# A hybrid encoder's first SSD layer with its time steps first, and the weight splits of the middle groups one unit further ahead

## The chip, the cores and the metric
The kernel runs on one core of a Trainium2 chip. The metric is the time of one execution on the device, in microseconds (us). TensorE is called PE in the rows of the profile (PEld is its weight load), VectorE is DVE, ScalarE is ACT, GpSimd is POOL, SyncE is SP.

## What is computed
An encoder trunk of four layers over 256 tokens of 1024 features, all in float32. The token mixers are, in order: a bidirectional Mamba-2 SSD, a short gated convolution, a neighbourhood attention and a second SSD. Each is followed by a dense MLP with squared ReLU, and each sub-layer by a LayerNorm. The SSD mixer, cut to what matters:
```python
zxbcdt = x @ w_in
z, xbc, dt_raw = split(zxbcdt)
xbc = silu(depthwise_conv(xbc, conv_w) + conv_b)
dt = softplus(dt_raw + dt_bias)            # the time steps, 2 directions x 32 heads
y = y_fwd + y_bwd + d_skip * xs            # y_fwd: chunks of 128 tokens, decays exp(cumsum(dt * a))
y = grouped_rmsnorm(y * silu(z), norm_w) @ w_out
```

## The kernel before
**Units.** All weights pass through SBUF in units of 128 x 2048 float32 (1 MB; the unit of the time steps, dt, has 0.26 MB). `plan_units` (L73) gives their order. Of an SSD layer there are, for each of 8 groups g, z(g), bc(g) (the state's two inputs), x(g) and, two groups later, so(g), the rows of the output weights. In the first layer the order is z0, z1, dt, bc0, x0, bc1, x1, z2, bc2, x2, so0, z3, bc3, x3, so1 and so on, units 0 to 14; the second layer has dt first. SyncE loads a unit with two DMAs into one of six raw buffers (RAW), when the unit six before it has been used up.

**Splits.** Every product is made of three in a reduced float32: high x high, high x low, low x high. ScalarE makes a unit's high part (`w_high`, a rounding copy, L1153) in one of five buffers, then VectorE the low part (`w_low`, raw minus high, L1568) in place of the raw unit. Both do it inside their own hand-written orders: `split_to(u)` makes all splits up to unit u that are still open. ScalarE waits for the unit's landing, VectorE for `w_high_done`. TensorE waits for both parts in `weights(u)`. Unit 0 alone is split in two halves with semaphores of their own (`first_high`, `first_low`, L1152, L1565), so that the first z product can begin with half of the weights. The products of one unit are 48 matmuls (L594 and L615), or 24 of 512 columns for so (L775).

**Start of the first layer.** TensorE turns x (L738), ScalarE and VectorE make its high and low parts (L1195, L1671), and TensorE then does z0, z1 with the turns of the parameters between their halves (`turn_ssd_parameters`, L820), dt (`dt_features`, L650), `turn_conv_parameters` (L828), `turn_dt` (L659), the first half of bc0 and so on. VectorE's `time_constants` (L1725 to L1742) are some twenty small dependent instructions that make softplus of dt; they need `a_done`, ScalarE's exponential of the parameter a (L1345), which waits for all parameter loads, SyncE's six and GpSimd's seven. Then come the cumulative sum on TensorE (`cumsum`, L883), its copies and decays, its turn (`cumsum_rows`, L891), a store to DRAM by ScalarE's queue (L1371) and GpSimd's broadcast loads of the decays (`load_decays`, L458).

**A middle group i (3 to 6).** TensorE: z(i), `state_products(i-1)` (L912), `turn_xs(i-1)` (L901), bc(i), `cross_chunk(i-1)` (L923), `scan(i-1)` (L936), x(i), so(i-2), `turn_gated(i-1)` (L947). VectorE: silu of z(i) (L1768), `decayed_products(i-1)` (L1797 to L1807), a split, `join_decays(i)` (L1786), `add_cross(i-1)` (L1817 to L1834), `taps` of bc(i) (L1756), `gate_scan(i-1)` (L1853, L1855), silu of bc(i), `rms_known(i-1)` (a wait for GpSimd's power, L481), a split, taps of x(i), silu of x(i), `gated_low(i-1)` (L1776), and the splits that end the loop. ScalarE: tanh of z(i), copies, a split, `shift_decays(i)` (L1269), `start_conv` of bc(i) (L1240, L1246), a split, tanh, `squares(i-1)` (L1311), decays, `normalise(i-1)` (L1319), start_conv of x(i), decays, a split, tanh, `gated_high(i-1)` (L1329), a split. The turns of the inner bank 1 (turn_xs, cross_chunk, turn_gated) wait for one another's readers, so turn_xs also waits for gated_low.

**How far the splits are ahead** is written out by hand. VectorE in a middle group before:
```python
split_to(names[("z", i)] + 4)
...
split_to(names[("bc", i)] + 4)
...
split_to(names[("x", i)] + 4)
if 2 < i < G - 2:
    split_to(names[("so", i - 2)] + 4)
```
With z3 as unit 11 this is 14 and 15, then 16, then 17 and 18, and for group 4: 19, 20, 21 and 22. In the tail (group 7) VectorE makes the split of so(4)+4 between `decayed_products(7)` and the silu of z(7).

## Time and profile before
| what | value |
|---|---|
| median of 3 runs | 1444.96 us (1442.81 to 1445.54) |
| the profiled execution's own time | 1442.69 us |
| its span, first to last instruction | 1441.0 us |
| TensorE matmuls busy | 1395.6 us, 97% of the span |
| VectorE busy | 1034.3 us, 72% |
| ScalarE busy | 763.0 us, 53% |
| mean granted TensorE clock | 0.993 of 2.4 GHz |
| the chain that ended last | TensorE 67%, VectorE 20%, ScalarE 5%, issue 5% |
| DMA | 266.86 MB, 185 GB/s on average |

A busy share is the time in which an engine had an instruction in work. Matmuls are pipelined and their ends are modelled, so TensorE's share is high wherever it doesn't wait. The share is an average over eight sub-layers (the first SSD layer takes about 250 us); a wait of TensorE is read in the stage where it stands.

### The profile page before, as it was taken

Reading aid. Unit: us, or ns where it says so; the run is one execution under the profiler, and the core shown is the slowest. Engines: PE = TensorE matmul, PEld = TensorE weight load, DVE = VectorE, ACT = ScalarE, POOL = GpSimd, SP = SyncE. Lnnn points to the kernel's source line nnn. Section 1 sums busy time; section 2 is a strip of 40 time slices with the busy share of each in tenths; the row PEclk is TensorE's granted clock in tenths of the full one; section 3 lists DMA queues with packets and bytes.
Section 4 is the critical chain, followed back from the end, with each engine's and each line's share of the span. In section 5 each row is a group of like instructions: output and inputs, shape, how many; then the busy total and the mean of one; then the engine's idle time right before and its main releaser. Section 6 shows DMA issues by size and latency. Waiting matters only on the chain.

```text
span 1441.0 us, 22905 instructions
## 1 busy us (share of the span) xinstructions
PE 1395.6 (97%) x8939; PEld 1261.0 (88%) x8939; DVE 1034.3 (72%) x1357; ACT 763.0 (53%) x1137; POOL 168.5 (12%) x229
## 2 busy tenths in 40 slices
PE   7999998999999999999999999999999999899996
PEld 7899997988889999888899798888998998798885
DVE  4899899666578486655766665656899899866554
ACT  4787776554434335444345444443587777554440
POOL 2121111622320000000000000000011121200000
PEclk9899999999999999999999999999999999999998
DMA  9756663676656556555554455554775664465550
GB/s 286 231 176 203 185 198 109 201 215 199 207 170 232 192 176 205 199 182 199 191 166 133 134 188 190 196 184 142 229 253 176 187 196 147 142 206 200 180 175 30
DMA packets 198474, 266.86 MB, mean 185 GB/s; under 512 B 11800, under 2 KB 167856, under 8 KB 198368
## 3 DMA queue, kind: packets, MB, share of 16 engines
q1 hardware_dynamic: 189008, 237.72, 50.8%
q0 software_dynamic: 9200, 27.55, 6.7%
q8 instruction: 72, 1.18, 0.3%
q14 instruction: 34, 0.28, 0.1%
q10 hardware_dynamic: 160, 0.13, 0.0%
HBM read 264.19 MB, written 1.18 MB: 184 GB/s over the span
## 4 chain that ended last, share of the span: by engine, by line
PE 67%; DVE 20%; ACT 5%; issue 5%; POOL 1%; DMA 0%; DVEq 0%; SPq 0%; ACTq 0%; POOLq 0%
PE y L775 27%; PE acc L594 12%; DVE conv L1756 6%; PE acc L632 6%; PE inner L632 6%; PE acc L615 5%; DVE w_low L1568 5%; PE inner L638 3%; PE acc L638 3%; PE y L615 2%; DVE E L1786 1%; ACT w_high L1153 1%; ACT E L1282 1%; PE inner L738 1%; DVE E L1834 1%
## 5 line engine op out<-in xcount | busy, mean ns | idle before, releaser
L1568 DVE TENSOR_TENSOR w_low<-raw,w_high 128x2048 fp32r<-128x2048 f32 (+1 forms) x226 | 511.0, 2270 | 52.5 <-ACT w_high L1153 40.7
L1153 ACT ACTIVATE w_high<-raw 128x2048 fp32r<-128x2048 f32 (+1 forms) x226 | 427.2, 1897 | 169.4 <-PE y L775 132.1
L775 PE MATMUL y<-w_high,opT 128*128 128x512 f32 x1408 | 397.0, 391 | 0.0
L594 PE MATMUL acc<-xT,w_high 128*128 128x256 f32 x1856 | 342.0, 286 | 1.0 <-DVE w_low L1568 0.8
L775 PEld LDWEIGHTS y<-w_high,opT 128*128 128x128 f32 x1408 | 259.3, 188 | 50.8 <-issue 0.7
L594 PEld LDWEIGHTS acc<-xT,w_high 128*128 128x128 f32 x1856 | 290.7, 193 | 2.8 <-issue 2.2
L594 PE MATMUL acc<-xT,w_low 128*128 128x256 f32 x928 | 263.3, 284 | 0.0
L775 PE MATMUL y<-w_low,opT 128*128 128x512 f32 x704 | 222.7, 390 | 0.0
L1587 DVE TENSOR_TENSOR opT<-conv,opT 128x512 fp32r<-128x512 f32 x56 | 40.4, 721 | 223.5 <-issue 202.2
L594 PEld LDWEIGHTS acc<-xT,w_low 128*128 128x128 f32 x928 | 178.8, 193 | 0.0
L615 PE MATMUL acc<-w_high,xT 128*128 128x256 f32 (+1 forms) x928 | 170.6, 286 | 3.4 <-DVE xT L1671 3.4
L775 PEld LDWEIGHTS y<-w_low,opT 128*128 128x128 f32 x704 | 132.1, 188 | 28.3
L615 PEld LDWEIGHTS acc<-w_high,xT 128*128 128x128 f32 x928 | 145.5, 193 | 4.5 <-issue 4.2
L632 PE MATMUL acc<-xT,w_high 128*128 128x512 f32 x352 | 136.9, 389 | 0.0
L632 PE MATMUL inner<-xT,w_high 128*128 128x512 f32 x352 | 136.9, 389 | 0.0
L615 PE MATMUL acc<-w_low,xT 128*128 128x256 f32 (+1 forms) x464 | 131.6, 284 | 0.0
L440 POOL TENSOR_TENSOR small<-small,minus_half 128x1 f32<-128x1 f32 x16 | 22.0, 1377 | 778.6 <-DVE small L1608 744.0
L1756 DVE SCALAR_TENSOR_TENSOR conv<-conv_pad,ssd_par,conv 128x256 f32<-128x256 f32 x256 | 105.6, 485 | 3.0 <-ACT conv L1246 3.0
L1214 ACT ACTIVATE conv<-acc 128x256 f32<-128x256 f32 x44 | 16.9, 384 | 153.6 <-PE inner L638 153.6
L615 PEld LDWEIGHTS acc<-w_low,xT 128*128 128x128 f32 x464 | 89.4, 193 | 0.0
L638 PE MATMUL inner<-xT,w_low 128*128 128x256 f32 x352 | 86.3, 283 | 0.0
L638 PE MATMUL acc<-xT,w_low 128*128 128x256 f32 x352 | 86.0, 282 | 0.0
(230 smaller groups left out, 1587.2 us busy)
## 6 DMA issues: line engine op xcount, KB each, us to landing
raw<-in_ffn_w_in SPq DMA_DIRECT2D x128, 512.0 KB, 4.7
raw<-in_ffn_w_out SPq DMA_DIRECT2D x128, 512.0 KB, 4.3
raw<-in_ssd_w_in SPq DMA_DIRECT2D x96, 512.0 KB, 5.1
E<-cumsum_dram POOLq DMA_DIRECT2D x32, 512.0 KB, 5.0
raw<-in_ssd_w_out SPq DMA_DIRECT2D x32, 512.0 KB, 4.4
raw<-in_sc_w_in SPq DMA_DIRECT2D x24, 512.0 KB, 4.7
raw<-in_na_w_qkv SPq DMA_DIRECT2D x24, 512.0 KB, 4.6
raw<-in_sc_w_out SPq DMA_DIRECT2D x8, 512.0 KB, 4.2
```

The lines of the kernel that those rows point to most:

```text
L440: nc.gpsimd.tensor_tensor(small[:, 2 + t:3 + t], small[:, t:t + 1], half_neg[:, 0:1], ALU.pow).then_inc(rstd_done, 1)
L594: mm = nc.tensor.matmul(bank[:, c * SEQ:(c + 1) * SEQ][:, span], w[:, col:col + P], xT[:, k, low, span], start=(k == 0 and part == 0), sto ...
L615: mm = nc.tensor.matmul(bank[:, t * width:(t + 1) * width], xT[:, k, low, t * P:(t + 1) * P], w[:, k * width:(k + 1) * width], start=(k == ...
L632: nc.tensor.matmul(wide_of[u][c][:, :], wh[:, col:col + P], xT[:, k, :, :].rearrange("p a b -> p (a b)"), start=(k == 0), stop=False)
L638: mm = nc.tensor.matmul(wide_of[u][c][:, 0:SEQ], wl[:, col:col + P], xT[:, k, 0, :], start=False, stop=(k == KT - 1))
L738: mm = nc.tensor.transpose(bank[:, q * P:(q + 1) * P], xs[:, t, c:c + P], ident[:, :])
L775: mm = nc.tensor.matmul(Y[t][c][:, :], opT[:, o % ACTS, low, k, t * P:(t + 1) * P], w[:, k * D + c * 512:k * D + (c + 1) * 512], start=(fi ...
L1153: nc.scalar.activation(w_high[:, u % SPLIT, c0:k * c], raw[:, u % RAW, c0:k * c], ACT.Copy).then_inc(w_high_done, 1)
L1214: ins = nc.scalar.activation(conv[:, o % 2, c, :], wide_of[names[("fi", b)]][c][:, SEQ:2 * SEQ], ACT.Copy)
L1568: V.tensor_tensor(w_low[:, u % RAW, c0:k * c], raw[:, u % RAW, c0:k * c], f(w_high[:, u % SPLIT, c0:k * c]), ALU.subtract).then_inc(w_low_ ...
L1587: V.tensor_tensor(low, src, high, ALU.subtract).then_inc(op_low, 1)
L1756: ins = V.scalar_tensor_tensor(out=y, in0=pad[:, c % 2, i, q:q + SEQ], scalar=tap(j, q, ct), in1=y, op0=ALU.mult, op1=ALU.add)
```

## The change
In the first SSD layer the unit of the time steps, dt, becomes unit 0 and z0 and z1 units 1 and 2. TensorE does dt first, then z0 and z1 with the turns and the cumulative sum between their halves, then bc0 and x0 whole. SyncE issues the second half of x in front of z0 and the six parameter loads in front of unit 2 rather than unit 3. ScalarE and VectorE follow in the same order; unit 0 is no longer split in halves (the semaphores `first_high` and `first_low`, with the code of `tokens` that waits for them, go). In the middle groups of both layers the three places of splits are z+5, bc+5 and x+5 (group 3: units 14, 15 and 16, then 17, then 18; group 4: 19 and 20, then 21, then 22), and the fourth goes. ScalarE's split before the tanh of x(i) goes with it. In the tail VectorE has one split less, between the products of group 7 and the silu of z(7); it is made at the end of group 6. The diff, with indentation cut:
```diff
@@ -83,14 +83,12 @@
 names = {}
 if kind == "ssd":
     for g in range(G + 2):
-        if g == 0 and j:
+        if g == 0:
             add(names, "dt", j, 0)
         if g < G - 1 and g != 1:
             add(names, "z", j, g)
         if g == 0:
             add(names, "z", j, 1)
-        if g == 0 and not j:
-            add(names, "dt", j, 0)
         if g < G:
             add(names, "bc", j, g)
             add(names, "x", j, g)
...
@@ -369,8 +366,8 @@
 for u in range(len(units)):
     if u == 1:
         sp.dma_start(xs[:, 1, :], x[0, P:2 * P, :]).then_inc(x_landed[1], 16)
+    if u == 2:
         sp.wait_ge(x_landed[0], 16)
-    if u == 3:
         load_parameters(sp, 0, par_landed[0])
     parts, k, n = weight_parts(u)
     if u >= RAW:
...
@@ -645,6 +634,9 @@
     bank = acc_bank((dt_copied, 1))
     n["dt"] += 1
     for k in range(KT):
+        if k % (KT // 2) == 0:
+            for t in range(NT):
+                x_half(0, t, k // (KT // 2))
         col = k * 2 * HEADS
         for part, (w, low) in enumerate(((wh, 0), (wh, 1), (wl, 0))):
             mm = nc.tensor.matmul(bank[0:2 * HEADS, 0:SEQ], w[:, col:col + 2 * HEADS], xT[:, k, low, :],
...
@@ -859,16 +851,11 @@
     if s == 0:
         for t in range(NT):
             turn_x(s, t)
-        bank = None
-        for t in range(NT):
-            bank = project(names[("z", 0)], [t], bank, arriving=(s, t))
-        bank = None
-        for t in range(NT):
-            bank = project(names[("z", 1)], [t], bank)
-            turn_ssd_parameters(t)
         dt_features(names[("dt", 0)])
-        turn_conv_parameters()
+        bank = project(names[("z", 0)], [0])
         turn_dt()
+        project(names[("z", 0)], [1], bank)
+        turn_ssd_parameters(0)
     else:
         head_units(s, [names[("dt", 0)], names[("z", 0)], names[("z", 1)]])
...
@@ -948,30 +935,25 @@
                                          gate_of(m)[:, t * GW + c * P:t * GW + (c + 1) * P], ident[:, :])
         mm.then_inc(op_turned, 1)
-    bank = acc_bank(freed_by("bc"))
-    features(names[("bc", 0)], bank, range(NT), None, [0])
     if s:
+        bank = acc_bank(freed_by("bc"))
+        features(names[("bc", 0)], bank, range(NT), None, [0])
         cumsum()
-    used(features(names[("bc", 0)], bank, range(NT), None, [1]))
-    if s:
+        used(features(names[("bc", 0)], bank, range(NT), None, [1]))
         cumsum_rows()
-        project(names[("x", 0)], range(NT))
     else:
+        bank = project(names[("z", 1)], [0])
+        turn_ssd_parameters(1)
         cumsum()
-        bank = acc_bank(freed_by("x"))
-        features(names[("x", 0)], bank, range(NT), None, [0])
+        project(names[("z", 1)], [1], bank)
+        turn_conv_parameters()
         cumsum_rows()
-        used(features(names[("x", 0)], bank, range(NT), None, [1]))
+        project(names[("bc", 0)], range(NT))
+    project(names[("x", 0)], range(NT))
     project(names[("bc", 1)], range(NT))
     state_products(0)
-    if s:
-        turn_xs(0)
-        project(names[("x", 1)], range(NT))
-    else:
-        bank = acc_bank(freed_by("x"))
-        features(names[("x", 1)], bank, range(NT), None, [0])
-        turn_xs(0)
-        used(features(names[("x", 1)], bank, range(NT), None, [1]))
+    turn_xs(0)
+    project(names[("x", 1)], range(NT))
     project(names[("z", 2)], range(NT))
     cross_chunk(0)
     scan(0)
...
@@ -1145,12 +1127,7 @@
     if u >= SPLIT:
         act.wait_ge(w_used, u - SPLIT + 1)
-    c0 = 0
-    if u == 0:
-
-        c0 = k * c // 2
-        nc.scalar.activation(w_high[:, 0, 0:c0], raw[:, 0, 0:c0], ACT.Copy).then_inc(first_high, 1)
-    nc.scalar.activation(w_high[:, u % SPLIT, c0:k * c], raw[:, u % RAW, c0:k * c],
+    nc.scalar.activation(w_high[:, u % SPLIT, 0:k * c], raw[:, u % RAW, 0:k * c],
                          ACT.Copy).then_inc(w_high_done, 1)
             def finished(u):
...
@@ -1335,40 +1312,44 @@
         tanh_of(bank[:, :], 0.5)
     if s == 0:
+        bank = finished(names[("dt", 0)])
+        nc.scalar.activation(csT[:, :], bank[0:2 * HEADS, 0:SEQ], ACT.Copy).then_inc(dt_copied, 1)
         split_to(2)
-        z_tanh(0)
-        split_to(3)
         for n_dmas, landed in zip(n_par_dmas, par_landed):
             act.wait_ge(landed, 16 * n_dmas)
         for q in range(n_ssd):
             ins = nc.scalar.activation(a_neg[:, q, :], a_neg[:, q, :], ACT.Exp)
         ins.then_inc(a_done, 1)
-        bank = finished(names[("dt", 0)])
-        nc.scalar.activation(csT[:, :], bank[0:2 * HEADS, 0:SEQ], ACT.Copy).then_inc(dt_copied, 1)
-        act.wait_ge(par_done, 2 * n_ssd + 1)
-    first = min(names[("dt", 0)], names[("z", 0)])
-    split_to(first + 3)
+    first = names[("dt", 0)]
+    if s:
+        split_to(first + 3)
     act.wait_ge(dt_biased, mixer + 1)
     nc.scalar.activation(dtt[:, 1, :, :], dtt[:, 0, :, :], ACT.Abs).then_inc(act_step, 1)
     n["step"] += 1
     act.wait_ge(act_step, n["step"])
     nc.scalar.activation(dtt[:, 2, :, :], dtt[:, 1, :, :], ACT.Exp, scale=-1.0).then_inc(dt_exp, 1)
-    split_to(first + 4)
+    split_to(first + (4 if s else 3))
     act.wait_ge(dt_floor, mixer + 1)
     nc.scalar.activation(dtt[:, 6, :, :], dtt[:, 7, :, :], ACT.Ln).then_inc(dt_log, 1)
-    split_to(first + 5)
+    split_to(first + (5 if s else 4))
+    z_tanh(0)
     if s:
-        z_tanh(0)
-    z_tanh(1)
+        z_tanh(1)
     act.wait_ge(ncs_done, mixer + 1)
     nc.scalar.activation(to_end[:, :, :], to_end[:, :, :], ACT.Exp)
     nc.scalar.activation(from_end[:, :, :].rearrange("p t c -> p (t c)"),
                          cs[:, :, :].rearrange("p t c -> p (t c)")[:, HEADS:3 * HEADS],
                          ACT.Exp).then_inc(ends_done, 1)
-    start_conv("bc", 0)
+    if s:
+        start_conv("bc", 0)
     act.wait_ge(cs_rows, mixer + 1)
     act.dma_start(rows_dram[j], csT[:, :]).then_inc(rows_stored, 16)
+    if not s:
+        z_tanh(1)
+        split_to(first + 5)
+        act.wait_ge(par_done, 2 * n_ssd + 1)
+        start_conv("bc", 0)
     split_to(first + 7)
     conv_tanh()
     start_conv("x", 0)
...
@@ -1399,7 +1380,7 @@
             if i == 3:
                 decays(2, early)
                 decays(2, late)
-            split_to(names[("z", i)] + 4)
+            split_to(names[("z", i)] + 5)
             shift_decays(i)
         start_conv("bc", i)
         if i == 2:
@@ -1415,18 +1396,16 @@
             split_to(names[("x", 2)] + 4)
             conv_tanh()
         else:
-            split_to(names[("bc", i)] + 4)
+            split_to(names[("bc", i)] + 5)
             conv_tanh()
             squares(i - 1)
             decays(i, early)
             normalise(i - 1)
             start_conv("x", i)
             decays(i, late)
-            split_to(names[("x", i)] + 4)
             conv_tanh()
             gated_high(i - 1)
-        if i > 2:
-            split_to(names[("so", i - 2)] + 4)
+            split_to(names[("x", i)] + 5)
     copy_cross(G - 2)
     copy_xs(G - 2)
     start_conv("bc", G - 1)
...
@@ -1876,27 +1849,28 @@
             dve.wait_ge(xs_turned, m - 1)
         silu(xsT[:, m % 2, :, :].rearrange("p a b -> p (a b)"), y)
+    def ssd_parameters(q):
+
+        dve.wait_ge(par_turned, q + 1)
+        bank = inner_of[("par", q)]
+        V.tensor_scalar(ssd_par[:, q, 0:TAPS + 1, :], bank[:, 0:(TAPS + 1) * CT]
+                        .rearrange("p (a b) -> p a b", b=CT), 0.5, None, ALU.mult).then_inc(par_done, 1)
+        V.tensor_copy(ssd_par[:, q, TAPS + 1, 0:DI // P],
+                      bank[:, (TAPS + 1) * CT:(TAPS + 1) * CT + DI // P]).then_inc(par_done, 1)
+
+    first = names[("dt", 0)]
     if s == 0:
         split_to(2)
+        dve.wait_ge(a_done, 1)
+        time_constants()
+        ssd_parameters(0)
+        split_to(3)
         silu_z(0)
-        split_to(3)
-        for q in range(n_ssd):
-
-            dve.wait_ge(par_turned, q + 1)
-            bank = inner_of[("par", q)]
-            V.tensor_scalar(ssd_par[:, q, 0:TAPS + 1, :], bank[:, 0:(TAPS + 1) * CT]
-                            .rearrange("p (a b) -> p a b", b=CT), 0.5, None, ALU.mult).then_inc(par_done, 1)
-            V.tensor_copy(ssd_par[:, q, TAPS + 1, 0:DI // P],
-                          bank[:, (TAPS + 1) * CT:(TAPS + 1) * CT + DI // P]).then_inc(par_done, 1)
-        dve.wait_ge(par_turned, n_ssd + 1)
-        V.tensor_copy(sc_par[:, :, :], inner_of[("par", n_ssd)][:, 0:SC_TAPS * KT]
-                      .rearrange("p (a b) -> p a b", b=KT)).then_inc(par_done, 1)
-        dve.wait_ge(par_done, 2 * n_ssd + 1)
-        dve.wait_ge(a_done, 1)
-    first = min(names[("dt", 0)], names[("z", 0)])
-    split_to(first + 3)
-    time_constants()
-    split_to(first + (5 if s else 4))
+        ssd_parameters(1)
+    else:
+        split_to(first + 3)
+        time_constants()
+        split_to(first + 5)
     dve.wait_ge(cs_acc, mixer + 1)
     sums = inner_of[("cs", j)]
     V.tensor_copy(cs[:, :, :], sums[:, 0:NT * 2 * HEADS].rearrange("p (t c) -> p t c", t=NT)).then_inc(cs_copied, 1)
...
@@ -1909,9 +1883,17 @@
                     ALU.add).then_inc(ncs_done, 1)
     if s:
         silu_z(0)
-    silu_z(1)
+        silu_z(1)
+    else:
+        split_to(4)
+        dve.wait_ge(par_turned, n_ssd + 1)
+        V.tensor_copy(sc_par[:, :, :], inner_of[("par", n_ssd)][:, 0:SC_TAPS * KT]
+                      .rearrange("p (a b) -> p a b", b=KT)).then_inc(par_done, 1)
     dve.wait_ge(cs_turned, mixer + 1)
     V.tensor_copy(csT[:, :], inner_of[("cs_rows", j)][0:2 * HEADS, 0:SEQ]).then_inc(cs_rows, 1)
+    if not s:
+        silu_z(1)
+        dve.wait_ge(par_done, 2 * n_ssd + 1)
     split_to(first + 5)
     y = taps("bc", 0)
     split_to(first + 6)
...
@@ -1950,19 +1932,17 @@
             gated_low(1)
             join_decays(2)
         else:
-            split_to(names[("z", i)] + 4)
+            split_to(names[("z", i)] + 5)
             join_decays(i)
             add_cross(i - 1)
             y = taps("bc", i)
             gate_scan(i - 1)
             silu_bc(i, y)
             rms_known(i - 1)
-            split_to(names[("bc", i)] + 4)
+            split_to(names[("bc", i)] + 5)
             silu_x(i, taps("x", i))
             gated_low(i - 1)
-        split_to(names[("x", i)] + 4)
-        if 2 < i < G - 2:
-            split_to(names[("so", i - 2)] + 4)
+        split_to(names[("x", i)] + (4 if i == 2 else 5))
     decayed_products(G - 2)
     y = taps("bc", G - 1)
     join_decays(G - 1)
@@ -1973,7 +1953,6 @@
     silu_x(G - 1, y)
     gate_scan(G - 2)
     decayed_products(G - 1)
-    split_to(names[("so", G - 4)] + 4)
     silu_z(G - 1)
     add_cross(G - 1)
```

## Rows read from the trace of the kernel before
**Rows 1.** Windows, all engines: start:end us, length, busy us (instructions), clock, DMA.
```profile
120.00:180.00 60.00, 59.26 (x432) 55.68 (x431) 52.95 (x82) 46.17 (x96) 11.21 (x12) 1.00 0.62 188
```

**Rows 2.** TensorE's waits, whole span: us in total, times, longest.
```profile
PE inner L901 <- DVE xsT L1768: 5.8, 4, 1.9
...
PE inner L947 <- ACT gate L1319: 1.4, 2, 0.7
```

**Rows 3.** Timeline, VectorE, a middle group: start us, us, line, [idle before <-releaser].
```profile
183.32 0.88 DVE L1776 SCALAR_TENSOR_TENSOR opT<-inner,ssd_par,opT 128x256 fp32r<-128x256 f32 x2
184.11 4.48 DVE L1568 TENSOR_TENSOR w_low<-raw,w_high 128x2048 fp32r<-128x2048 f32 x2
188.51 0.68 DVE L1768 SCALAR_TENSOR_TENSOR ring_c<-tanh,acc 128x512 f32<-128x512 f32 x1
...
203.15 2.29 DVE L1568 TENSOR_TENSOR w_low<-raw,w_high 128x2048 fp32r<-128x2048 f32 x1 [1.45 <-POOL small L481]
...
210.39 0.88 DVE L1776 SCALAR_TENSOR_TENSOR opT<-inner,ssd_par,opT 128x256 fp32r<-128x256 f32 x2
```

**Rows 4.** Timeline, TensorE, where it waits or nearly waits in the first layer.
```profile
122.95 0.44 PE L947 MATMUL inner<-ident,gate 128*128 128x128 f32 x2 [0.72 <-ACT gate L1319]
...
211.63 0.38 PE L901 MATMUL inner<-ident,xsT 128*128 128x128 f32 x2
...
226.29 0.55 PE L901 MATMUL inner<-ident,xsT 128*128 128x128 f32 x3 [1.92 <-DVE xsT L1768]
...
239.77 0.33 PE L947 MATMUL inner<-ident,E 128*128 128x128 f32 x1 [1.33 <-ACT E L1319]
```

**Rows 5.** Timeline, VectorE, the splits of group 3.
```profile
107.71 4.49 DVE L1568 TENSOR_TENSOR w_low<-raw,w_high 128x2048 fp32r<-128x2048 f32 x2
```

**Rows 6.** Timeline, ScalarE, the split behind `gated_high`.
```profile
183.18 1.91 ACT L1153 ACTIVATE w_high<-raw 128x2048 fp32r<-128x2048 f32 x1
```

**Rows 7.** Timeline, VectorE's split and ScalarE's tanh of z in the tail.
```profile
229.42 2.28 DVE L1568 TENSOR_TENSOR w_low<-raw,w_high 128x2048 fp32r<-128x2048 f32 x1
...
229.85 0.60 ACT L1254 ACTIVATE tanh<-acc 128x512 f32<-128x512 f32 x1 [1.35 <-PE acc L615]
```

**Rows 8.** The start: SyncE's and GpSimd's issues (timeline), then one load's us to landing.
```profile
4.38 0.37 SPq L383 DMA_DIRECT2D raw<-in_ssd_w_in  x1
...
6.97 2.03 SPq L353 DMA_DIRECT2D E<-in_ssd_conv_w  x1
...
11.71 0.44 SPq L387 DMA_DIRECT2D raw<-in_ssd_w_in  x1
...
9.83 0.79 POOL L353 DMA_DIRECT2D E<-in_ssd_conv_w  x1 [6.26 <-DMA x_tokens<-in_x]
...
13.29 0.60 POOL L423 DMA_DIRECT2D E<-in_sc_conv_w  x1
...
E<-in_sc_conv_w POOLq DMA_DIRECT2D x1, 12.0 KB, 7.9
```

**Rows 9.** Timeline, VectorE: time constants (first, last), first taps, first decayed products.
```profile
28.80 0.29 DVE L1725 TENSOR_TENSOR xsT<-inner,dt_bias 128x128 f32<-128x128 f32 x1 [0.44 <-PE inner L659]
...
35.05 0.28 DVE L1742 SCALAR_TENSOR_TENSOR xsT<-dts,a_neg 128x128 f32<-128x128 f32 x1
...
44.96 3.24 DVE L1756 SCALAR_TENSOR_TENSOR conv<-conv_pad,ssd_par,conv 128x256 f32<-128x256 f32 x8
...
66.46 1.22 DVE L1801 TENSOR_TENSOR E<-E,inner 128x1024 f32<-128x1024 f32 x1
```

**Rows 10.** Windows: bc0's matmuls alone (PE, PEld, clock), then all around the cumulative sum.
```profile
28.60:34.60 6.00, 6.00 (x48) 5.81 (x48) 1.00 0.97 326
...
34.60:37.69 3.09, 1.54 (x14) 1.45 (x13) 3.06 (x6) 2.50 (x3) 0.00 (x0) 0.95 1.16 311
```

**Rows 11.** Windows around two waits of TensorE: the column behind POOL is the clock.
```profile
38.00:40.00 2.00, 2.00 (x11) 2.00 (x11) 1.10 (x3) 1.96 (x6) 0.00 (x0) 0.50 1.16 312
224.00:226.00 2.00, 0.38 (x2) 0.00 (x0) 1.90 (x4) 1.20 (x4) 0.00 (x0) 1.00 0.00 0
```

More of the change, by code:

```diff
@@ L250, in build @@
         w_high_done, w_low_done, w_used = sem("w_high_done"), sem("w_low_done"), sem("w_used")
-        first_high, first_low = sem("first_high"), sem("first_low")
         consts, par_turned, par_done, a_done = sem("consts"), sem("par_turned"), sem("par_done"), sem("a_done")
@@ L599, in tokens @@
             def tokens(u, bank, ts, arriving, width, ks=range(KT)):
-                if u == 0 and 0 in ts:
-                    pe.wait_ge(first_high, 1)
-                    pe.wait_ge(first_low, 1)
-                    wh, wl = w_high[:, 0, :], w_low[:, 0, :]
-                else:
-                    wh, wl = weights(u)
+                wh, wl = weights(u)
                 for t in ts:
                     for k in ks:
-                        if u == 0 and t == 0 and k == KT // 2:
-                            weights(u)
                         if arriving and k % (KT // 2) == 0:
@@ L949, in turn_gated @@
                         mm.then_inc(op_turned, 1)
-                    bank = acc_bank(freed_by("bc"))
-                    features(names[("bc", 0)], bank, range(NT), None, [0])
                     if s:
+                        bank = acc_bank(freed_by("bc"))
+                        features(names[("bc", 0)], bank, range(NT), None, [0])
                         cumsum()
-                    used(features(names[("bc", 0)], bank, range(NT), None, [1]))
-                    if s:
+                        used(features(names[("bc", 0)], bank, range(NT), None, [1]))
                         cumsum_rows()
-                        project(names[("x", 0)], range(NT))
                     else:
+                        bank = project(names[("z", 1)], [0])
+                        turn_ssd_parameters(1)
                         cumsum()
-                        bank = acc_bank(freed_by("x"))
-                        features(names[("x", 0)], bank, range(NT), None, [0])
+                        project(names[("z", 1)], [1], bank)
+                        turn_conv_parameters()
                         cumsum_rows()
-                        used(features(names[("x", 0)], bank, range(NT), None, [1]))
+                        project(names[("bc", 0)], range(NT))
+                    project(names[("x", 0)], range(NT))
                     project(names[("bc", 1)], range(NT))
                     state_products(0)
-                    if s:
-                        turn_xs(0)
-                        project(names[("x", 1)], range(NT))
-                    else:
-                        bank = acc_bank(freed_by("x"))
-                        features(names[("x", 1)], bank, range(NT), None, [0])
-                        turn_xs(0)
-                        used(features(names[("x", 1)], bank, range(NT), None, [1]))
+                    turn_xs(0)
+                    project(names[("x", 1)], range(NT))
                     project(names[("z", 2)], range(NT))
@@ L1560, in split_to @@
                     dve.wait_ge(raw_landed[u % RAW], 32 * (u // RAW + 1))
-                    c0 = 0
-                    if u == 0:
-                        c0 = k * c // 2
-                        dve.wait_ge(first_high, 1)
-                        V.tensor_tensor(w_low[:, 0, 0:c0], raw[:, 0, 0:c0], f(w_high[:, 0, 0:c0]),
-                                        ALU.subtract).then_inc(first_low, 1)
                     dve.wait_ge(w_high_done, u + 1)
-                    V.tensor_tensor(w_low[:, u % RAW, c0:k * c], raw[:, u % RAW, c0:k * c],
-                                    f(w_high[:, u % SPLIT, c0:k * c]), ALU.subtract).then_inc(w_low_done, 1)
+                    V.tensor_tensor(w_low[:, u % RAW, 0:k * c], raw[:, u % RAW, 0:k * c],
+                                    f(w_high[:, u % SPLIT, 0:k * c]), ALU.subtract).then_inc(w_low_done, 1)
             def finished(u):
```

## The prediction, made before the changed kernel ran

> **What bounds the kernel now.** I first read TensorE's own waits and the windows of a stage in the middle of the first SSD layer. Between 120 and 180 us TensorE is busy 59.26 of 60 us and VectorE 52.95 [rows 1], so there TensorE looks like the bound. But its waits over the whole program name VectorE: 5.8 us in four waits of the transposes of xs (L901) and 1.4 us in two of the turn of the gated values (L947, `turn_gated`) [rows 2]. Then I read VectorE instruction by instruction through one middle group [rows 3]. From the end of one `gated_low` (L1776) to the next is 27.07 us (183.32 to 210.39), of which about 3 us is idle, 1.45 of them behind GpSimd's power. That idle time is latency inside a loop: gate, ScalarE's squares, GpSimd's power, ScalarE's normalise. None of it waits for a projection. So VectorE's order free-runs at 27.07 us per group, beside a TensorE whose own period must be about the same, as it idles 0.74 us in 60. Where the order got late it shows on TensorE: 0.72 us at 122.95, 1.92 us at 226.29 and 1.33 us at 239.77 in the first layer [rows 4], and by the counts of [rows 2] the same in the second. **The reader should see that VectorE's sequence, not its busy share, sets the end of both SSD layers.** Any time that is inserted into it comes out at 226.29.
>
> **The change, part by part.** No arithmetic is added or removed: the matmuls, the splits (1.9 us on ScalarE, 2.29 on VectorE) and the bytes are the same. Splitting unit 0 in two goes, which saves two small instructions. All that counts is order.
>
> *Middle groups, the third split.* At group 3 the old order makes two splits (units 14, 15) before `join_decays`, the new one three. VectorE's pair takes 4.49 us [rows 5], so a third adds 2.25 us ahead of taps, `gate_scan(2)`, the squares and `turn_gated(2)`, where TensorE already waits 0.72 us [rows 4]. Nothing covers it. From then on the order stays one unit further ahead, and never gives this back. Cost 2.25 us in each SSD layer, +4.5. Unit 16's load is issued when unit 10 is done (about 94 us), ten microseconds ahead, so I cost SP's queue at nothing; ScalarE's third split (1.9 us) falls into the time in which VectorE makes its own three.
>
> *Middle groups, the end of the loop.* The old order has two splits there on VectorE (184.11, 4.48 us) [rows 3]. The first is of a unit whose high part ScalarE made before the tanh of x, so it starts at once. The second's high part is made at 183.18 to 185.09, after `gated_high` [rows 6], and is hidden by the first. The new order leaves only the second. VectorE comes to it at 184.11 and finds it ready at 185.1: a new wait of 1.0 us. Behind the waiting instruction are queued silu of z, the decayed products, two splits, and so everything of the next group. Groups 3, 4, 5 and 6 have it, in two layers: 8 times 1.0 = +8.0. What would cover it is TensorE's being later still; the 1.92 us wait at 226.29 says that it isn't. The decayed products come 2.3 - 1.0 us earlier, but TensorE's scan doesn't wait for them now, so this gains nothing.
>
> *Tail.* Between the products of group 7 and its silu of z stood one split, 229.42 to 231.70. It goes. ScalarE's tanh of z is ready at 230.45 [rows 7], so silu starts at 230.5 and not where the split ends: 1.1 us of 2.28 is gained, and it reaches `turn_gated(7)`, where TensorE waits 1.33 us [rows 4]. What is late next is TensorE itself. Twice -1.1 = -2.2.
>
> *Start.* Unit 0 becomes dt (0.26 MB instead of 1.05). x's first half lands at 4.4 [rows 8]; the second, now behind 1.3 MB and not 2.1, by the same rate (1.57 MB in the 5 us to 9.8, when GpSimd starts behind it) near 7. SP's six parameter issues move from 6.97 (where they end at 11.7) to 4.4, in front of z1, which so is issued near 9.1 instead of 4.38, and unit 3 near 10. GpSimd's seven issues start 2.4 to 2.8 us earlier; their last landed at 13.29 + 7.9 = 21.2, now near 18.8. ScalarE's exponential of a (0.4) follows. VectorE has z1's low part at 19.0. So the time constants start near 19.2, not 28.80; they take 6.5 us (28.80 to 35.33) [rows 9] and end at 25.7. On TensorE z0 can't start before its whole low part (z0 lands near 10, plus 1.9, plus 2.3: 14.6), with dt before it. After z0's 6.0 us, half of z1 and the small turns it reaches the cumulative sums near 24.5 and waits till 26.1, since their bank is freed by the parameters behind the time constants: 1.6 us, as much as the old waits around the sums together (3.09 us with 1.5 busy) [rows 10]. Then sums 1.5, half of z1 3.0, small turns 0.7 and bc0 6.0 [rows 10] end at 37.3, or 1.5 us later if the clock falls. It does now: after 3.1 us of waits and small matmuls (34.6 to 37.69) the granted clock was 0.50, the 1.2 GHz level, at 38 to 40 [rows 10, 11]. I take 38.8. ScalarE's pad and first taps (1.7) let VectorE's first taps start at 40.6, against 44.96 [rows 9]. ScalarE's tanh of z0 (behind unit 4's split and a table load) and its row DMA all lie before that. **Of 9.6 us at the time constants only 4.4 are left at the taps, because bc0 now comes behind the whole cumulative sum and ends 4 us later than before (34.6).** From taps to the first decayed products (44.96 to 66.46) VectorE has the same list and hardly idles, so the 4.4 stay. Bounds: 0 if bc0's lateness takes it all, 7 if parameters land at once.
>
> **Sum**: -4.4 + 4.5 + 8.0 - 2.2 = **+5.9 us**. The profiled execution took 1442.69 us (span 1441.0), so it would take 1448.6; the median of the runs shown is 2.3 us above it, and from that I forecast **1450.9**. Bounds: lead 0 to 7 gives +10.3 to +3.3; a wait of 0.8 to 1.2 for each 1.0 adds -1.6 to +1.6.
>
> **A rule and a row.** At group 3 TensorE would idle about 0.7 + 2.25 = 2.9 us. In the rows 1.92 us of idleness (224 to 226) left the clock at 1.00, and 3.1 us before 37.69 left it at 0.50 [rows 11]; 2.9 lies nearer to the second. At half clock 11 matmuls ran in 2 us against 16 (48 in 6.0 us) [rows 10, 11]: over some 5 us 1.5 us are lost per dip. I leave it out of the sum, as VectorE is by then the later engine, and the 3 us by which its silu (188.51 [rows 3]) comes after z's tanh (right behind the split that ends at 185.09) take the delay.
> The Trainium skill, "TensorE: Matmul & The Clock Gate", Part 1, says that an idle array falls back to 1.2 GHz and must earn 2.4 GHz again. By that rule each of these two stalls brings a dip; the rows of 37.69 agree, those of 226.29 don't.
>
> **Rivals.**
> 1. *The forecast, slower*: 60%.
> 2. *The start gives little* (parameters as late as today, a further clock dip that is not absorbed): lead 0 to 2, +8.3 to +10.3, or +1.5 us in each layer, +8.9: 1453 to 1455. For it: both of its queues, SP's and GpSimd's, are moved at once. 15%.
> 3. *The other side, faster*: the middle is paced by TensorE, and the inserted waits fill idle time of VectorE (7 of 60 us [rows 1]). It decides if VectorE's `gated_low` came 1 us or more before TensorE's next transpose; now it ends at 211.27 and the transpose starts at 211.63, 0.4 us before it, and at 226.29 silu of x is 1.9 after TensorE [rows 3, 4]. The middle is then worth 0 and the sum -4.4 - 2.2 = -6.6: 1438.4. 13%.
> 4. *Nothing to measure*: the lead at the start is 7 to 9 us, because the clock doesn't fall and the parameters land early. +1.3 to +3.3: 1447. 12%.
> That the change doesn't do what it says I exclude: all of it is order on queues that the diff shows.
>
> **Numbers.** A measurement of this kernel tells about 0.2% (2.9 us) from no change: faster is under 1442.1, slower over 1447.9. Faster 0.13, same 0.14 (case 4 and the edge of 1), slower 0.73. Range 1443 to 1456.5: it takes in cases 1, 2 and 4 with their bounds, and leaves out case 3 and the farthest edge.
>
> **What would show it.** Right: on VectorE a wait of about 1.0 us for the high part before the split that follows `gated_low`, in groups 3 to 6 of both layers; their period 28.1 and not 27.07 us; TensorE waiting about 2.9 us at the first `turn_gated` with a wait and 0.9 us at each later xs transpose; the tail from the transpose at 226.29 to `turn_gated(7)` 1.1 us shorter; first decayed products near 62. Wrong: the period stays at 27.07, or VectorE's first taps start before 38 or after 43.

## The result, and the profile after

The changed kernel takes 1454.95 us (median of 4 runs, 1453.83 to 1456.94) against 1444.03 for the kernel before (4 runs beside it): ratio 1.0078 [1.0067, 1.009]. It is slower by 10.9 us. The forecast was 1450.9, in a range of 1443 to 1456.5.

The profiled execution took 1453.88 us, with a span of 1452.1 (before 1441.0). TensorE is busy 1400.2 us (96%), VectorE 1036.2 (71%), ScalarE 763.0 (53%), and the granted clock is 0.992. The totals hardly move. Of the 11.1 us that the span grew, 6.5 are idle time of TensorE (45.4 us before, 51.9 now) and 4.6 are time in which its matmuls took longer. Line numbers have moved: `w_low` is L1541 now (L1568 before), `w_high` L1130 (L1153), `gated_low` L1749 (L1776), `turn_xs` L888 (L901), `turn_gated` L934 (L947), the taps L1729 (L1756).

TensorE's waits over the whole span (total, times, longest), which answer to [rows 2]:
```profile
PE inner L888 <- DVE xsT L1741: 9.2, 5, 3.1
PE inner L934 <- ACT gate L1296: 8.6, 7, 2.9
...
PE inner L870 <- DVE ssd_par L1858: 2.7, 1, 2.7
```
The waits of `turn_gated` for the normalised gate go from 1.4 us in two to 8.6 us in seven, and the cumulative sums (L870) have a wait of 2.7 us.

VectorE's timeline in the same middle group as [rows 3]:
```profile
186.65 0.88 DVE L1749 SCALAR_TENSOR_TENSOR opT<-inner,ssd_par,opT 128x256 fp32r<-128x256 f32 x2
188.52 2.29 DVE L1541 TENSOR_TENSOR w_low<-raw,w_high 128x2048 fp32r<-128x2048 f32 x1 [0.99 <-ACT w_high L1130]
190.73 0.68 DVE L1741 SCALAR_TENSOR_TENSOR ring_c<-tanh,acc 128x512 f32<-128x512 f32 x1
...
214.81 0.88 DVE L1749 SCALAR_TENSOR_TENSOR opT<-inner,ssd_par,opT 128x256 fp32r<-128x256 f32 x2
```
One split follows `gated_low` and not two, and it stands behind a wait of 0.99 us. From `gated_low` to `gated_low` it is now 28.16 us (186.65 to 214.81), not 27.07. ScalarE's timeline says what VectorE waits for; its high part ends at 188.4 and was begun only behind `gated_high` (L1306):
```profile
185.79 0.82 ACT L1306 ACTIVATE opT<-inner,ssd_par 128x256 fp32r<-128x256 f32 x2
186.50 1.91 ACT L1130 ACTIVATE w_high<-raw 128x2048 fp32r<-128x2048 f32 x1
```
VectorE at group 3, where three splits stand in a row (two in [rows 5]):
```profile
106.60 6.69 DVE L1541 TENSOR_TENSOR w_low<-raw,w_high 128x2048 fp32r<-128x2048 f32 x3
```
TensorE's timeline at the places of [rows 4], first layer, then the same two in the second:
```profile
124.06 0.89 PE L934 MATMUL inner<-ident,gate 128*128 128x128 f32 x4 [2.93 <-ACT gate L1296]
...
208.53 0.66 PE L934 MATMUL inner<-ident,gate 128*128 128x128 f32 x4 [0.62 <-ACT gate L1296]
...
231.73 0.66 PE L888 MATMUL inner<-ident,xsT 128*128 128x128 f32 x4 [3.13 <-DVE xsT L1741]
...
244.19 0.66 PE L934 MATMUL inner<-ident,E 128*128 128x128 f32 x4 [0.33 <-ACT E L1296]
...
1230.60 1.12 PE L888 MATMUL inner<-ident,xsT 128*128 128x128 f32 x4 [3.13 <-DVE xsT L1741]
...
1244.41 0.66 PE L934 MATMUL inner<-ident,E 128*128 128x128 f32 x4 [0.30 <-ACT E L1296]
```
The wait of 0.72 us became 2.93, and that of 1.92 us 3.13. The waits that the later groups have now are small and stand at `turn_gated`, 0.33 to 0.62 us each. The tail of the first layer, 226.29 to 239.77 before, is 231.73 to 244.19: 12.46 us and not 13.48. That of the second, 1219.41 to 1232.90 before, is 1230.60 to 1244.41: 13.81 us, and not shorter.

The start, VectorE's time constants (L1698), first taps and first decayed products, which answer to [rows 9]:
```profile
21.24 0.28 DVE L1698 TENSOR_TENSOR xsT<-inner,dt_bias 128x128 f32<-128x128 f32 x1
...
43.94 3.26 DVE L1729 SCALAR_TENSOR_TENSOR conv<-conv_pad,ssd_par,conv 128x256 f32<-128x256 f32 x8 [1.75 <-ACT conv L1223]
...
65.45 1.22 DVE L1774 TENSOR_TENSOR E<-E,inner 128x1024 f32<-128x1024 f32 x1
```
The time constants come 7.6 us earlier than before, the taps only 1.0, and so do the decayed products. Between the two lie TensorE's cumulative sums:
```profile
28.20 0.38 PE L870 MATMUL inner<-xsT,prefix 128*128 128x32 f32 x2 [2.68 <-DVE ssd_par L1858]
```
In windows (as [rows 10] and [rows 11]; the last three numbers are the clock, the DMA engines' busy share and GB/s), the DMA system at the start, the clock behind the sums, and the clock behind three waits of about 3 us:
```profile
8.00:10.00 2.00, 1.35 (x7) 0.98 (x7) 1.34 (x3) 1.20 (x2) 2.00 (x4) 1.00 0.85 243
10.00:12.00 2.00, 2.00 (x11) 2.00 (x10) 0.37 (x1) 1.62 (x1) 1.76 (x4) 1.00 0.18 49
...
30.00:36.00 6.00, 6.00 (x31) 5.75 (x31) 4.33 (x9) 1.95 (x4) 0.00 (x0) 0.53 0.88 280
...
124.00:128.00 4.00, 3.94 (x21) 3.94 (x22) 3.74 (x7) 2.75 (x8) 0.00 (x0) 0.57 0.62 164
1122.00:1126.00 4.00, 3.06 (x26) 3.06 (x27) 3.74 (x5) 3.64 (x10) 0.00 (x0) 1.00 0.88 239
1230.00:1234.00 4.00, 3.40 (x17) 3.40 (x18) 3.75 (x10) 1.39 (x5) 1.40 (x3) 0.57 0.00 0
```
From 10 to 12 us the DMA engines are busy 18% of the time, at 49 GB/s. The clock was at the 1.2 GHz level from 30 on, after 124 and after 1230, but at full speed behind the 2.93 us before 1122.94.

**The balance** from the traces, by what each stretch grew. First layer: start -1.0 (decayed products 66.46 to 65.45), group 3 +2.2 (`gated_low(1)` to `gated_low(2)`: 28.25 to 30.48), four waits at the loop's end +4.3 (three in periods of 28.15 for 27.05, the fourth between the last `gated_low` of the loop and the transposes of xs), tail -1.0: in sum +4.5, and the turn of x at its end moves from 252.38 to 256.77, +4.4. Second layer: +2.2, +4.3, +0.3: the same turn moves from 1245.85 to 1257.01, another +6.8 (between these stretches +0.3 ahead of group 3 and -0.35 behind the tail cancel).

### The profile page after: what moved, and what is told of

Read it like the earlier page. It is cut to its first block, busy times and chain, and to the rows that moved or that the text cites. A ratio compares the mean times of both kernels' runs of the same rounds, so it can differ in the third digit from the quotient of the medians.

```text
span 1452.1 us, 22899 instructions
## 1 busy us (share of the span) xinstructions
PE 1400.2 (96%) x8939; PEld 1262.7 (87%) x8939; DVE 1036.2 (71%) x1356; ACT 763.0 (53%) x1136; POOL 163.7 (11%) x229
## 4 chain that ended last, share of the span: by engine, by line
PE 65%; DVE 19%; issue 7%; ACT 7%; POOL 1%; DMA 1%; SPq 0%; DVEq 0%; ACTq 0%; POOLq 0%
PE y L767 26%; PE acc L591 11%; DVE conv L1729 6%; PE inner L621 5%; PE acc L621 5%; PE acc L604 5%; DVE w_low L1541 3%; PE inner L627 3%; PE acc L627 3%; PE y L604 2%; ACT w_high L1130 2%; DVE E L1759 1%; ACT E L1259 1%; DVE E L1807 1%; PE inner L730 1%
## 5 line engine op out<-in xcount | busy, mean ns | idle before, releaser
L1541 DVE TENSOR_TENSOR w_low<-raw,w_high 128x2048 fp32r<-128x2048 f32 (+1 forms) x226 | 512.2, 2276 | 61.7 <-ACT w_high L1130 49.9
L1130 ACT ACTIVATE w_high<-raw 128x2048 fp32r<-128x2048 f32 (+1 forms) x226 | 427.4, 1902 | 165.6 <-PE y L767 129.9
L1729 DVE SCALAR_TENSOR_TENSOR conv<-conv_pad,ssd_par,conv 128x256 f32<-128x256 f32 x256 | 105.9, 488 | 4.8 <-ACT conv L1223 4.8
```

The source lines that it names most:

```text
L1130: nc.scalar.activation(w_high[:, u % SPLIT, 0:k * c], raw[:, u % RAW, 0:k * c], ACT.Copy).then_inc(w_high_done, 1)
L1541: V.tensor_tensor(w_low[:, u % RAW, 0:k * c], raw[:, u % RAW, 0:k * c], f(w_high[:, u % SPLIT, 0:k * c]), ALU.subtract).then_inc(w_low_don ...
L1729: ins = V.scalar_tensor_tensor(out=y, in0=pad[:, c % 2, i, q:q + SEQ], scalar=tap(j, q, ct), in1=y, op0=ALU.mult, op1=ALU.add)
```

## The experiments

The kernel before took 1443.97 us beside the first four (13 runs) and 1443.89 beside the other four (20 runs).

**Only the start** of the change: middle groups and tail are put back to those of before (the edit of the next experiment, reversed).


> The changed kernel with the middle groups and the tail as before. Theory A (the middle's splits cost all, the start gives 1.0 us): 1.0 us under before, 1443; first decayed products 1.0 us earlier, VectorE's period in groups 3 to 6 back at 27.07 us. Rival B (the start costs, by a cold clock and late loads, and the middle little): 5 us or more over before.


Measured: 1442.65 us (10 runs), ratio 0.9995 [0.9985, 1.0005]. In a trace the sums wait 2.83 us at 29.02, and the waits of the middle are those of before (0.74, 1.91 us). The start is worth 1.3 us by the medians, not 4.4, and the interval (-2.2 to +0.7 us) doesn't tell it from nothing. In this trace the first decayed products come at 66.28, 0.2 us earlier than before; in that of the changed kernel it was 1.0. Rival B is refuted.

**Only the middle and the tail**, in the kernel before:
```diff
-split_to(names[("z", i)] + 4)
+split_to(names[("z", i)] + 5)
...
-split_to(names[("bc", i)] + 4)
+split_to(names[("bc", i)] + 5)
...
-split_to(names[("x", i)] + 4)
-if 2 < i < G - 2:
-    split_to(names[("so", i - 2)] + 4)
+split_to(names[("x", i)] + (4 if i == 2 else 5))
...
-split_to(names[("so", G - 4)] + 4)
 silu_z(G - 1)
```
(ScalarE's order likewise.)


> The kernel before with only the splits of the middle groups and the tail changed. Theory A: both layers pay 2.2 us for the third split and 4 times 1.08 us for the wait of VectorE's split, and get 1.0 us back in the tail: 11 to 12 us over before, 1456. Rival B: under 5 us over before.


Measured: 1458.05 us (4 runs, 1454.93 to 1459.48), ratio 1.0097 [1.0081, 1.0113]: +14.1. TensorE's waits are those of the changed kernel (2.91 at 127.92, 3.11 at 235.59). All of the loss is in this part. It is 1.8 us more than the +12.3 that the balance gives for its stretches, which four runs can't resolve; in its trace 2.1 us are lost ahead of the first decayed products (68.54 against 66.46), where nothing was changed.

**The high part in time**: the changed kernel, but ScalarE makes the split of x+5 before the tanh of x(i).
```diff
 decays(i, late)
+split_to(names[("x", i)] + 5)
 conv_tanh()
 gated_high(i - 1)
-split_to(names[("x", i)] + 5)
```


> The changed kernel, but ScalarE makes the high part of unit x+5 before its tanh of x, where the kernel before has a split, not after gated_high. Theory A (what costs is VectorE's wait for the high part): the wait of 0.99 us in groups 3 to 6 of both layers is gone, the period is 27.07 us again, and the time falls by 8 to 10 us, to about 1446; the transposes of group 7 wait 1.9 us or less, and the clock doesn't fall there. Rival C (what costs is being one unit further ahead as such, by loads or buffers): under 2 us.


Measured: 1449.28 us (4 runs), ratio 1.004 [1.0025, 1.0055]: 5.7 us less than the changed kernel. VectorE's timeline of it:
```profile
131.01 0.87 DVE L1749 SCALAR_TENSOR_TENSOR opT<-inner,ssd_par,opT 128x256 fp32r<-128x256 f32 x2
131.80 2.28 DVE L1541 TENSOR_TENSOR w_low<-raw,w_high 128x2048 fp32r<-128x2048 f32 x1
...
158.01 0.88 DVE L1749 SCALAR_TENSOR_TENSOR opT<-inner,ssd_par,opT 128x256 fp32r<-128x256 f32 x2
...
235.14 0.69 DVE L1741 SCALAR_TENSOR_TENSOR ring_c<-tanh,acc 128x512 f32<-128x512 f32 x1 [2.59 <-ACT tanh L1231]
```
The wait is gone and the period is 27.00 us, as before: the wait was the whole of the 1.1 us per group. But only 5.7 us come back, and not the 8 to 10 expected. The trace shows two losses at the end of the layer. First, TensorE's clock fell behind the wait of 2.93 us at 124.74 (0.50 from 126 to 128 us), and in the second layer behind that of 2.92 us at 1124.25 too, and TensorE has no wait behind it until the tail. There VectorE waits for conv and tanh of bc7, where it didn't before:
```profile
217.57 3.26 DVE L1729 SCALAR_TENSOR_TENSOR conv<-conv_pad,ssd_par,conv 128x256 f32<-128x256 f32 x8 [0.23 <-ACT conv L1223]
...
223.43 0.69 DVE L1741 SCALAR_TENSOR_TENSOR ring_a<-tanh,conv 128x512 f32<-128x512 f32 x1 [0.80 <-ACT tanh L1231]
```
The stretch from the last `gated_low` of the loop to the transposes of xs takes 17.17 us in both layers, against 15.9 before. That this is the late TensorE is argued from these waits, not shown alone. Second, behind the transposes the clock fell once more in the first layer. TensorE's transposes, then a window behind them:
```profile
229.34 0.66 PE L888 MATMUL inner<-ident,xsT 128*128 128x128 f32 x4 [1.91 <-DVE xsT L1741]
```
```profile
230.00:234.00 4.00, 4.00 (x23) 4.00 (x23) 2.52 (x8) 1.51 (x5) 1.93 (x3) 0.57 0.01 4
```
So VectorE's silu of z7 waits 2.59 us, and from the transposes to `turn_gated(7)` it takes 13.95 us; in the second layer, with the clock at 1.00, it takes 12.45. The whole stretch from the last `gated_low` of the loop (212.17) to the next (241.39) is 29.22 us against 27.48 before and in the changed kernel. The expectation that the clock wouldn't fall there was wrong.

**The third split one group later**: the same, with group 3's places left at +4.


> As high_before_tanh, but group 3 keeps two splits, one and the pair at its end; the three splits in a row fall into group 4. Theory A (each layer pays one split once, wherever it stands): the same time as high_before_tanh within 1 us; TensorE waits about 0.7 us at the turn of the gated values of group 3 and the missing 2.2 us at that of group 4. Rival D (only group 3, where the order is late already, pays): 3 us or more under high_before_tanh.


Measured: 1452.74 us (4 runs), ratio 1.0061 [1.0046, 1.0076]. TensorE waits 0.74 us at 121.75 (group 3, as before), then 1.36 at 130.38 and 2.03 at 153.15. The split's cost moves with it and doesn't go away, so rival D is refuted. But the time isn't that of the kernel above within 1 us: by the medians it is 3.5 us dearer. The edit moves more than one split. At the end of group 3 ScalarE now makes two high parts (3.70 us, from 124.39) ahead of the tanh of x, so VectorE's silu of x waits 2.11 us where it waits 0.77 elsewhere:
```profile
128.71 0.69 DVE L1741 SCALAR_TENSOR_TENSOR xsT<-tanh,conv 128x512 f32<-128x512 f32 x1 [2.11 <-ACT tanh L1231]
```
That gives the new wait of 1.36 us at 130.38, and 1.35 at 1129.88 in the second layer. Counted from `gated_low(1)`, the transposes of group 7 come 0.8 us later in each layer than in the kernel above. That is 1.6 of the 3.5 us; the rest is open, as the two profiled executions have the same span, 1449.1 us.

**The sums behind z1**: `start_only`, with
```diff
 bank = project(names[("z", 1)], [0])
 turn_ssd_parameters(1)
-cumsum()
 project(names[("z", 1)], [1], bank)
+cumsum()
+bank = acc_bank(freed_by("bc"))
+features(names[("bc", 0)], bank, range(NT), None, [0])
 turn_conv_parameters()
 cumsum_rows()
-project(names[("bc", 0)], range(NT))
+used(features(names[("bc", 0)], bank, range(NT), None, [1]))
```


> start_only (which took 1442.65 us, the kernel before 1443.97), and in it TensorE's cumulative sums no longer stand between the two halves of z1 but behind the whole of z1, and their turn between the two halves of bc0; VectorE's and ScalarE's orders stay. Theory A (the lead was lost at the sums: TensorE waited 2.7 to 2.8 us there, and then made the second half of z1 at half clock, 5.5 us instead of 3.0): z1's second half fills the wait, bc0's first half ends near 33.5, the whole of it near 37 to 38 instead of 42.1 to 43, VectorE's first taps start near 39 to 40 instead of 43.9, and the time falls by 3 us or more, to 1439.5 or less. Theory B (the lead was lost to z1's late landing at 17.0 and everything follows from there): the wait at the sums only moves, bc0 comes as late as now, and the time stays within 1 us of start_only, 1442 to 1443.5. Theory C: bc0 does come earlier, but the next late thing takes its place (splits of units 4 and 5 on VectorE, or their landing), so that the first decayed products come less than 1.5 us earlier.


Measured: 1439.99 us (11 runs), ratio 0.9976 [0.9965, 0.9987], 2.7 us less than `start_only`. No wait at the sums, and the clock is 1.00 from 26 to 44 us. VectorE's first taps start at 42.02 without a wait: right behind its own split of a unit, which itself waits 1.14 us for the high part. TensorE is so early now that it waits 2.90 us for the first xs, at 52.76. By place theory A holds: bc0's first half ends near 33.9 and the whole of it near 37.4. Its sizes are not quite reached: the taps were to start near 39 to 40, and the time was to fall by 3 us. The first decayed products come at 64.64, 1.6 us earlier than in `start_only`, so that theory C, the next late thing, takes the rest.

**The parameters behind z1's load**: `start_only`, with
```diff
 if u == 2:
     sp.wait_ge(x_landed[0], 16)
+if u == 3:
     load_parameters(sp, 0, par_landed[0])
```


> start_only, and in it SyncE's six parameter loads stand behind the load of z1 again (in front of unit 3), so z1 is issued 3 us earlier. Theory A (z1 landed at 17.0, 9.9 us after its issue, because it stood behind the small parameter packets on a nearly idle DMA system): z1 lands near 12 to 14, VectorE's low part of it starts near 15.5 and not 19.0, and the time constants start when the exponential of a is there, near 20 instead of 21.2; the sums come up to 1.2 us earlier, their wait shrinks by as much, and the time falls by about 1 us, to 1441.6. Theory B (the parameters are what the time constants wait for, and they now come as much later as z1 comes earlier): nothing, 1442 to 1443.5, with the time constants at 21 to 22.


Measured: 1440.41 us (10 runs), ratio 0.9975 [0.9962, 0.9987], 2.2 us less than `start_only`. Its windows at the start and behind the sums, and then its timeline:
```profile
10.00:12.00 2.00, 2.00 (x11) 2.00 (x10) 0.44 (x1) 1.47 (x1) 1.83 (x4) 1.00 1.10 346
...
28.00:32.00 4.00, 4.00 (x23) 4.00 (x23) 2.52 (x9) 1.91 (x3) 0.00 (x0) 0.59 1.09 362
```
```profile
19.61 0.28 DVE L1701 TENSOR_TENSOR xsT<-inner,dt_bias 128x128 f32<-128x128 f32 x1
...
26.58 0.38 PE L871 MATMUL inner<-xsT,prefix 128*128 128x32 f32 x2 [1.00 <-DVE ssd_par L1861]
...
62.27 1.22 DVE L1777 TENSOR_TENSOR E<-E,inner 128x1024 f32<-128x1024 f32 x1
```
From 10 to 12 us the DMA engines move 346 GB/s; in `start_only` it was 154 and in the changed kernel 49. ScalarE begins z1's high part at 15.40 without a wait for its landing (17.85 in `start_only`, behind a wait of 1.98). The time constants start at 19.61, the wait is 1.00 us (the clock falls behind it all the same, to 0.59), and the lead at the first decayed products is 4.2 us (66.46 to 62.27). I had expected half of this gain.

**Both**.


> Both of these edits to start_only. If the sums' wait with its cold clock is the cause and z1's landing adds to it: the sum of the two, about -4 us against start_only, 1438.5. If either of them only moves a wait: no better than the better one of them alone.


Measured: 1439.03 us (5 runs), ratio 0.9965 [0.9952, 0.9978], the best kernel here, 4.9 us below the one before. Against `start_only` it is 3.6 us less, where the two edits alone gave 2.7 and 2.2. It is 1.0 us below the better of the two, which their intervals don't tell apart: in part they remove the same wait. What is late next is VectorE (TensorE waits 2.10 us for the first xs at 52.24, and 1.92 and 1.36 in the tail as ever).

**Filling VectorE's idle time**: `start_only`, with
```diff
-rms_known(i - 1)
 split_to(names[("bc", i)] + 4)
+rms_known(i - 1)
```


> start_only, and in the middle groups VectorE makes the split of bc before it waits for GpSimd's power of the normalisation, not behind that wait; it needs nothing of the power itself. In the kernel before it idles 1.45 us there in each group. Theory A (VectorE's sequence of 27.07 us is what sets TensorE's waits of 0.7, 1.9 and 1.3 us in each SSD layer): the split fills the idle time, VectorE's period is held by TensorE alone, the waits of 1.9 us at the transposes of xs go, and the time falls by 3 to 6 us below start_only, to 1437 to 1440. Theory B (GpSimd's power is slowed while VectorE makes a split, or the split holds up the low part of the gated values): the normalisation comes later, TensorE's wait at the turn of the gated values grows from 0.74 us, and the time stays or rises, 1442 to 1448.


Measured: 1456.03 us (5 runs), ratio 1.0085 [1.0069, 1.01]: 13.4 us slower than `start_only`. GpSimd's timeline in `start_only`, then VectorE's and GpSimd's in this kernel:
```profile
120.66 0.19 POOL L477 TENSOR_SCALAR small<-small 128x2 f32<-128x2 f32 x1 [8.56 <-ACT square L1288]
120.94 0.72 POOL L478 TENSOR_TENSOR small<-small,minus_half 128x2 f32<-128x2 f32 x1
```
```profile
119.69 2.28 DVE L1543 TENSOR_TENSOR w_low<-raw,w_high 128x2048 fp32r<-128x2048 f32 x1
125.50 3.26 DVE L1731 SCALAR_TENSOR_TENSOR conv<-conv_pad,ssd_par,conv 128x256 f32<-128x256 f32 x8 [3.52 <-ACT conv L1223]
```
```profile
120.21 1.82 POOL L477 TENSOR_SCALAR small<-small 128x2 f32<-128x2 f32 x1 [8.57 <-ACT square L1288]
122.11 0.72 POOL L478 TENSOR_TENSOR small<-small,minus_half 128x2 f32<-128x2 f32 x1
```
GpSimd's instruction of 0.19 us takes 1.82 and ends where VectorE's split ends (121.97 and 122.03). The same stands in all eight groups. ScalarE's normalise and all behind it come later, VectorE idles 3.52 us for the next conv, and its period is 28.73 us (130.18 to 158.91) and not 27.05. About 1.7 us in each of the eight groups make up the 13.4.

## Why the prediction was right, and where it was not

**Direction and place were right, the size was nearly half too small**: slower by 10.9 us (1454.95 against 1444.03 beside it), where the sum had 5.9. The mechanism was rival 1: VectorE's sequence, not its busy share. The time came out closer (4.1 us off) than the sum (5.0 off), since the kernel before took 1444.03 us beside it and not the 1445.0 from which I had started. That is luck. By term:

- *Third split*, +2.25 per layer: measured +2.2 in VectorE's list in each layer, and TensorE's wait of 2.93 us where 2.9 was worked out. `ahead_from_group4` shows that it costs where it stands. Right.
- *The wait at the end of the loop*, 8 x 1.0: measured 0.98 to 0.99 us of idle time at 8 places, and 1.1 per period, 8.6 in all. The remaining 0.1 is overlap: in [rows 3] the split begins 0.09 us before the end of the instructions ahead of it, and behind a wait it can't. `high_before_tanh` removes it and gets the period back. Right; but I placed the visible waits at the transposes of xs, and they stand at `turn_gated` (0.3 to 0.6 us each).
- *Tail*, 2 x -1.1: first layer -1.0, second +0.3. **A step that failed**: no clock dip was priced behind the transposes of xs. Behind the same wait of 3.13 us the clock in the second layer fell (0.57 from 1230 to 1234), in the first it stayed at 1.00 (TensorE had 19 matmuls in the 2 us from 232). The four kernels with this tail (the changed one, `middle_only`, `high_before_tanh`, `ahead_from_group4`) show it eight times: from the transposes to `turn_gated(7)` it takes 12.45 or 12.46 us where the clock stays at 1.00 (four times) and 13.81 to 13.97 where it falls to 0.50 (four times). So the edit itself gives 1.0 us, as worked out, and a dip takes 1.4 to 1.5 us. The sum lacked 1.4 us there.
- *Start*, -4.4: measured -1.0 in the changed kernel's trace, -0.2 in that of `start_only`. **This is the term that was mis-sized most, by 3.4 us.** Two of its steps failed. The prediction had z1's low part "at 19.0" and the time constants "near 19.2"; the low part was not finished at 19.0 but begun (19.03), since z1, issued at 7.16, landed at 17.0. The six small loads of SyncE stood before it in its queue, GpSimd's were issued beside it, and the DMA system was nearly idle (49 GB/s from 10 to 12 us). I counted those loads as issue time of a queue, not as time in which the big load behind them doesn't move. So the wait at the sums was 2.68 us and not 1.6. And then the clock fell behind that wait, so that half of z1 took 5.5 us and not 3.0 plus 1.5. `start_par_behind_z1` gives 4.2 us at the first decayed products (4.4 were forecast), with a wait of 1.00, and 2.2 us of the kernel's time, and `start_sums_later` gets 2.7 us by taking sums and wait out of the way. Both causes are shown; they overlap.
- *A rule and a row.* The first 2.93 us wait brought a dip (0.57), the same wait in the second layer none (1.00), so the row that I chose doesn't foretell the single case. Nor was 1.92 us of waiting a safe row: the same wait ahead of the first layer's transposes brought a fall in `start_only`, `high_before_tanh`, `ahead_from_group4` and `start_par_behind_z1`, and none in the kernel before. The Trainium skill, "TensorE: Matmul & The Clock Gate", Part 1, ties the fall to an idle stretch that is long enough; it doesn't say that each stall brings one. "By that rule each of these two stalls brings a dip" was read into it. As forecast, VectorE covered the first dip: z4 took 7.4 us and not 6.0 (124.61 to 131.98), and nothing came out of it while VectorE was later. In `high_before_tanh` that cover is gone.

With -1.0 for -4.4, +8.6 for +8.0 and -0.7 for -2.2 the sum is +11.4, against 11.1 us between the spans and 10.9 between the medians.

Rival 2 (the start gives little, +8.3 to +10.3, 1453 to 1455) came nearest in size, and had 15%: it was the forecast's own mechanism with the start near its lower bound. Rival 3 is refuted by `middle_only`: TensorE doesn't pace the middle.

**Open.** Why the clock fell behind one wait of 2.93 us and not behind the other wasn't tried. Nor was what `high_before_tanh` would give without its dips. `start_only` and `middle_only` add up to 12.8 us by their medians, 10.9 were measured.

## What to carry to other kernels

Where an engine free-runs through an order written by hand, count what each moved instruction waits for at its new place: here the second of two splits hid a high part of 1.9 us, and without the first it cost 1.1 us in each of 8 groups. A load's issue time doesn't say when it moves: here a 1 MB load behind six small ones in its queue landed 9.9 us after its issue, so try the one that gates a wait first. Price a clock dip as a chance, not as a yes or no. And idle time ahead of a wait is not free room: look at who works in it before you fill it.

## What the runs showed of the hardware that I had not expected

- **VectorE's split shuts GpSimd out.** A 0.19 us instruction of GpSimd took 1.82 us beside a split of 2.28, in each group. The wait for GpSimd's power, which looks like 1.45 us of idle time, keeps them apart, and taking it away cost 13.4 us. The Trainium skill, "SBUF — State Buffer", says that VectorE and GpSimd share a port pair, that a VectorE operation with two SBUF inputs holds it for its whole length against a GpSimd instruction that reads SBUF, and that the other fully blocks. The trace agrees. The kernel before had the sign of it in its tail: the same instruction of GpSimd takes 1.22 us at 236.78 and ends (238.00) with VectorE's split (235.67 to 237.96).
- **The DMA system nearly idle behind small loads.** While some 13 parameter loads of 8 to 80 KB were under way, it moved 49 GB/s from 10 to 12 us in the changed kernel, and 346 with the 1 MB unit issued ahead of them. The kernel before has such a lull too, 40 GB/s from 13 to 14 us. Which of the small loads or of the two queues makes it was not tried.
- **Equal waits, unequal clocks.** Waits of 2.68, 2.90, 2.93 and 3.13 us brought the 1.2 GHz level, and so did four of 1.9 us in first layers' tails and one of 1.00 us with small matmuls behind it; another 2.93, another 3.13, the 2.03 us at 153.15 of `ahead_from_group4` and the seven waits of 1.9 us in the second layers' tails didn't. Among the 20 later executions of the kernel before, the three slowest (1447.8 to 1447.9) have a mean clock of 0.990 and the fastest (1440.73) 0.994, so such dips are probably part of that spread; with one execution of each kernel traced, this isn't shown.
